# Gated delta rule in a two-block kernel: the block inverse in 64x64 tiles, and the next round's front ordered between the state products

## The reference, cut to what matters

```python
g = jnp.cumsum(g, axis=-1)
decay = jnp.exp(jnp.where(incl, g[..., :, None] - g[..., None, :], -jnp.inf))
kb = k * beta
a_mat = jnp.where(strict, jnp.einsum('bhncd,bhnsd->bhncs', kb, k) * decay, 0.0)
rhs = jnp.concatenate([v * beta, kb * jnp.exp(g)[..., None]], axis=-1)
sol = lax.linalg.triangular_solve(eye + a_mat, rhs, left_side=True, lower=True, unit_diagonal=True)
...
v_new = u_i - jnp.einsum('bhcd,bhdv->bhcv', w_i, state)
o_i = q_i @ state + qk_i @ v_new
state = state * jnp.exp(gl_i)[..., None, None] + jnp.einsum('bhcd,bhcv->bhdv', k_i, v_new)
```

## Time and profile before

| | us |
|---|---|
| median of 3 runs | 2495.45 |
| lowest and highest | 2495.17, 2495.8 |
| the profiled execution | 2499.06 |
| its span | 2497.1 |
| PE busy (share of the span) | 2319.3 (93%) |
| DVE busy | 966.6 (39%) |
| ACT busy | 752.4 (30%) |
| POOL busy | 1029.2 (41%) |
| the recurrence, from the first L1242 to the end of its last product | 322.9 to 674.9 |

### The profile page before, as it was taken

One profiled execution on the slowest core, in us unless ns is written; L12 is line 12 of the kernel. 1 busy time (PEld: TensorE's weight loads), 2 busy tenths in 40 slices (PEclk: granted clock), 3 DMA queues, 4 the chain that ended last, 5 costly groups with the idle time before them and its releaser, 6 DMA issues.

```text
span 2497.1 us, 40813 instructions
## 1 busy us (share of the span) xinstructions
PE 2319.3 (93%) x16316; PEld 1846.6 (74%) x16316; DVE 966.6 (39%) x1715; ACT 752.4 (30%) x1151; POOL 1029.2 (41%) x471
## 2 busy tenths in 40 slices
PE   6998787878798999999999999999999999898999
PEld 2787655666666887887887888887888887547999
DVE  4459554555546122124346112124112113855212
ACT  2443412222223222222222322322322322424444
POOL 1445511132243443443443444443444443303888
PEclk8999776787898999999999999999999999989999
DMA  6233433432452422222432432222432222202555
GB/s 241 93 110 127 152 124 133 161 146 109 178 205 77 169 93 88 98 93 76 154 116 68 160 110 94 93 99 79 143 111 97 97 93 85 73 0 76 186 178 184
DMA packets 82706, 297.78 MB, mean 119 GB/s; under 512 B 9072, under 2 KB 11504, under 8 KB 82288
## 3 DMA queue, kind: packets, MB, share of 16 engines
q1 hardware_dynamic: 82400, 295.03, 34.4%
q10 hardware_dynamic: 144, 0.34, 0.0%
HBM read 294.28 MB, written 1.05 MB: 118 GB/s over the span
## 4 chain that ended last, share of the span: by engine, by line
issue 52%; PE 22%; POOL 19%; DVE 6%; ACT 1%; POOLq 1%; DVEq 0%; ACTq 0%
POOL w_lo L509 19%; PE bank L533 3%; PE bank L534 3%; PE bank L537 3%; PE bank L1292 1%; PE bank L1273 1%; PE bank L577 1%; PE bank L908 1%; DVE gdn_blocks L1510 1%; PE bank L1349 1%; PE bank L2053 1%; PE bank L2054 1%; PE bank L1356 1%; PE bank L2094 1%; PE bank L1281 0%
## 5 line engine op out<-in xcount | busy, mean ns | idle before, releaser
L509 POOL TENSOR_TENSOR w_lo<-w_raw,w_hi 128x1024 fp32r<-128x1024 f32 x383 | 934.3, 2443 | 1181.7 <-ACT w_hi L761 1181.3
L533 PE MATMUL bank<-n_hi,w_lo 128*128 128x512 f32 (+1 forms) x2216 | 796.4, 359 | 38.6 <-POOL w_lo L509 19.5
L537 PE MATMUL bank<-n_lo,w_hi 128*128 128x512 f32 (+1 forms) x2216 | 793.4, 358 | 0.6 <-DVE n_lo L685 0.4
L534 PE MATMUL bank<-n_hi,w_hi 128*128 128x512 f32 (+1 forms) x2216 | 790.4, 357 | 0.0
L761 ACT CAST w_hi<-w_raw 128x1024 fp32r<-128x1024 f32 x383 | 401.1, 1049 | 782.1 <-PE bank L537 771.9
L533 PEld LDWEIGHTS bank<-n_hi,w_lo 128*128 128x128 f32 x2216 | 424.6, 192 | 119.5 <-issue 46.4
L534 PEld LDWEIGHTS bank<-n_hi,w_hi 128*128 128x128 f32 x2216 | 425.0, 192 | 68.2 <-issue 3.6
L537 PEld LDWEIGHTS bank<-n_lo,w_hi 128*128 128x128 f32 x2216 | 424.5, 192 | 66.1 <-DVE n_lo L685 2.6
L1861 DVE TENSOR_TENSOR prod<-silu,bank 128x512 f32<-128x512 f32 (+1 forms) x88 | 54.4, 620 | 731.7 <-PE bank L537 724.3
L537 PE MATMUL bank<-g_lo,w_hi 128*128 128x512 f32 (+1 forms) x768 | 284.6, 371 | 0.0
L533 PE MATMUL bank<-g_hi,w_lo 128*128 128x512 f32 (+1 forms) x768 | 283.0, 369 | 1.1 <-DVE g_lo L1852 1.1
(11 more groups left out here) (314 smaller groups left out, 2018.0 us busy)
## 6 DMA issues: line engine op xcount, KB each, us to landing
w_raw<-in_stream SPq DMA_DIRECT2D x383, 512.0 KB, 3.4
mod_raw<-in_modstream SPq DMA_DIRECT2D x64, 512.0 KB, 4.5
late<-in_modstream SPq DMA_DIRECT2D x56, 512.0 KB, 4.7
w_raw<-in_modstream SPq DMA_DIRECT2D x48, 512.0 KB, 7.0
h<-in_tokens SPq DMA_DIRECT2D x1, 2048.0 KB, 10.7
consts<-in_consts SPq DMA_DIRECT2D x1, 1152.0 KB, 8.6
h<-in_ctx SPq DMA_DIRECT2D x1, 1024.0 KB, 8.2
out<-h SPq DMA_DIRECT2D x8, 128.0 KB, 3.4
```

The lines of the kernel that those rows point to most:

```text
L509: nc.gpsimd.tensor_tensor(w_lo[:, slot, :], w_raw[:, slot, :], w_hi[:, slot, :].bitcast(F32), ALU.subtract).then_inc(w_lo_ready, 1)
L533: nc.tensor.matmul(out_ap, wl, hi, start=start, stop=False)
L534: nc.tensor.matmul(out_ap, wh, hi, start=False, stop=False)
L537: return nc.tensor.matmul(out_ap, wh, lo, start=False, stop=stop)
```

## The change

In the inverse, levels 1 to 4 work on the two 64x64 diagonal blocks instead of the four 32x32 ones. `ac`, `atc`, `xc` and `xtc` are 256 wide instead of 128, and half as many products of twice the size are issued. The first three level masks are applied by DVE (level 1) and POOL (2 and 3, and 4 once the slot of 2 is free). `x_half` and POOL's spreading into `xt` are gone; level 6 reads `xc` and `xtc`, and ACT copies the two diagonal blocks into `xt`. The gram is multiplied by the mask first (from PSUM) and by the decay later (in SBUF).

The next round's front moves into this round: its sums stand behind keys by state, its gram behind the new values, its transposed keys behind the state update, and DVE, ACT and POOL follow. The outputs and the state update now use bank `b0+2`, and the transposed keys `b0`. The slots of the modulation parts in a round are now four, two and six. Of the decay's argument, FWD's is made by ACT (four Relu with a bias of -cum) and BWD's by DVE (subtract, max). The argument for the queries' decay is made by ACT from PSUM.

```diff
-    MOD_SLOTS = {"gram": 6, "at": 0, "level1": 0, "level2": 0, "level3": 0, "level4": 0, "level5": 0, "level6": 0,
-                 "state": 4, "out": 2}
+    MOD_SLOTS = {"state": 4, "out": 2, "gram": 6}
...
+                    at_li = w["ac"] if li == 1 else w["atl"][:, li % 2]
                     for j in range(4):
-                        for i in range(4):
-                            last = nc.tensor.matmul(packed(b0 + 2, blk(i))[:, j], w["atl"][blk(i), li - 1, j],
-                                                    w["xc"][blk(i), j], start=True, stop=True)
+                        for i in range(2):
+                            last = nc.tensor.matmul(packed(b0 + 2, half(i))[:, j], at_li[half(i), j], w["xc"][half(i), j],
+                                                    start=True, stop=True)
...
+        for r, (step_, hg) in enumerate(ROUNDS):
+            inverse(r)
             for n, d, t, hs, b0, gc in batches:
                 if step_:
                     pe.wait_ge(d_state, n - 3)
...
+            if r + 1 < len(ROUNDS):
+                sums(r + 1)
             some_mods(r, "state")
...
+                pe.wait_ge(a_xt, n + 1)
                 four(lambda j: nc.tensor.matmul(b4(b0 + 2)[:, j], w["xt"][:, j], w["rhs"][:, j],
                                                 start=True, stop=True), g_vn)
+            if r + 1 < len(ROUNDS):
+                gram(r + 1)
...
+                    four(out_four, g_o)
             some_mods(r, "out")
...
+                    four(lambda j: nc.tensor.matmul(b4(b0 + 2)[:, j], w["ktok"][:, j], w["rhs"][:, j],
                                                     start=True, stop=True), g_st)
+            if r + 1 < len(ROUNDS):
+                key_rows(r + 1)
+            some_mods(r, "gram")
         mod_turn(pe, RECUR_LAST)

     def act_recur(act):
+        def decay(r):
+            for n, d, t, hs, b0, gc in per_batch(r):
+                if d == BWD:
+                    act.wait_ge(d_relu, r + 1)
+                else:
...
+                        last = nc.scalar.activation(w["dec"][:, j], b4(b0)[:, j], ACT.Relu,
+                                                    bias=neg_cum[:, t, gc.start + j:gc.start + j + 1])
...
+                nc.scalar.activation(w["dec"][:], w["dec"][:], ACT.Exp, scale=-1.0).then_inc(a_dec, 1)
+        def query_decay(r):
...
+                if m >= 2:
+                    act.wait_ge(g_o, m - 1)
+                nc.scalar.activation(w["qdec"][:], b4(b0), ACT.Exp).then_inc(a_qd, 1)
+                for j in range(4):
+                    last = nc.scalar.activation(w["pt"][:, j], b4(b0)[:, j], ACT.Relu, scale=-1.0,
+                                                bias=cum[:, t, gc.start + j:gc.start + j + 1])
...
     def pool_recur(pool):
-                tt(w["atl"][:, 1:4], w["atc"].unsqueeze(1).to_broadcast([P, 3, 4, BLK]),
-                   packed_level[1 - d][:, 2:5].unsqueeze(2).to_broadcast([P, 3, 4, BLK]), ALU.mult).then_inc(p_at, 1)
+                pool.wait_ge(d_a, n + 1)
+                tt(w["atl"], w["atc"].unsqueeze(1).to_broadcast([P, 2, 4, PAIR]),
+                   packed_level[1 - d][:, 1:3].unsqueeze(2).to_broadcast([P, 2, 4, PAIR]), ALU.mult).then_inc(p_at, 1)
-                tt(w["xt"][:].rearrange("p j (i c) -> p j i c", i=4), w["xtc"].unsqueeze(2).to_broadcast([P, 4, 4, BLK]),
-                   own_block.unsqueeze(1).unsqueeze(3).to_broadcast([P, 4, 4, BLK]), ALU.mult).then_inc(p_diag, 1)
...
     def dve_recur(dve):
+        def masked_gram(r):
+                nc.vector.scalar_tensor_tensor(w["a"][:], b4(b0 + 1), -1.0, w["t1"][:],
+                                               ALU.mult, ALU.mult).then_inc(d_gm, 1)
+        def first_blocks(r):
+                dve.wait_ge(d_gm, n + 1)
+                dve.wait_ge(a_dec, n + 1)
+                for i in range(2):
+                    last = tt(w["ac"][half(i)], w["a"][half(i), :, half(i)], w["dec"][half(i), :, half(i)], ALU.mult)
+                step(last)
+                step(tt(w["xc"], w["ac"], first_level[d].unsqueeze(1).to_broadcast([P, 4, PAIR]), ALU.mult))
+                nc.vector.transpose(flat(w["atc"]), flat(w["ac"])).then_inc(d_atc, 1)
+                tt(w["xc"], w["xc"], packed_ident.unsqueeze(1).to_broadcast([P, 4, PAIR]), ALU.add).then_inc(d_xm, 1)
+                tt(w["ac"], w["atc"], packed_level[1 - d][:, 0].unsqueeze(1).to_broadcast([P, 4, PAIR]),
+                   ALU.mult).then_inc(d_at, 1)
+                nc.vector.transpose(flat(w["xtc"]), flat(w["xc"])).then_inc(d_xt, 1)
+                tt(w["a"][:], w["a"][:], w["dec"][:], ALU.mult).then_inc(d_a, 1)
+        def decay_argument(r):
+            n, d, t, hs, b0, gc = per_batch(r)[BWD]
+            step(tt(w["dec"][:], b4(b0), bc(cum[:, t, gc]), ALU.subtract))
+            nc.vector.tensor_scalar(w["dec"][:], w["dec"][:], 0.0, None, ALU.max).then_inc(d_relu, 1)
```

382 lines of the change are left out of this document (205 added, 177 removed).

## The result

The changed kernel takes 2466.8 us (median of 4 runs, 2465.04 to 2467.92) against 2495.62 for the kernel before in the same comparison: a ratio of 0.988, with an interval of 0.9863 to 0.9897. It is 28.8 us faster. The prediction was 2484.6, with a range of 2467 to 2502: the sign was right, but the time lies just under the range, and the gain is more than twice the forecast 10.8.

A forecast was written before the change was run, and what follows sets the result against it. In levels 1 to 4 PE was taken to wait for its instruction stream. Terms -13.2 + 8.1 - 4.8 - 5.6 + 1 + 3.7 = -10.8 us gave 2488.3 for the profiled execution, 2484.6 for the median; range 2467 to 2502.

The forecast's parts named there:

- Levels 1 to 4: Inverse levels in the recurrence: halved instructions should end PE's wait for its instruction stream, 104.0 to 90.8 us, -13.2.
- I take 3.0, the middle: Time per level in levels 1 to 4, taken as 3.0 us between the full-clock and half-clock prices.
- Full clock: Levels 1 to 4 with PE at full clock: the chain bounds a level, at 2.5 us; -27 for the stage.
- Half clock: Levels 1 to 4 at half clock: PE bounds a level, 3.4 us; throughout, as rival, 2498 us, chance 0.17.
- full clock in the levels: Rival: new products keep PE busy 70% or more of a level, stages cost 14 less, 2471 us; chance 0.12.
- Levels 5 and 6: Inverse's last levels: L1535 leaves DVE and L1474 leaves POOL, shortening the way to L1333, -4.8 us.
- First products: Start of each round until both directions have their first block: PE waits for DVE, 39.9 to 48 us, +8.1.
- the front between the state products: Next round's sums, gram and key transposes fill PE's holes between state products, -5.6 us (bounds 0 and -8).
- The charge for collisions: First products: one DVE collision with POOL of 0.85 us a round; as rival, four a round, 2505 us, chance 0.17.
- Modulation parts: Loads for each round's last six parts, now needed some 10 us after the state slot instead of 13: +1 us.
- The joint: Recurrence to output projection: last six parts move behind the outputs, L611 later, squares faster, +3.7 us (0 to +8).
- The backward argument on DVE: BWD's decay argument, about 1.1 us before L1573, covered by four parts and L1356; uncovered 1.1 a round.

The follow-up runs named there:

- the run with the late front: Changed kernel with the next round's sums and gram back behind the state update on all engines, tiles still 64x64: 2466.27 us.
- the run with half the products: Changed kernel with levels 1 to 4 on 32-row tiles, only blocks 0 and 2 of four issued, 128 PE instructions a level: 2492.66 us.
- the small loads: Changed kernel with each modulation load in the recurrence, from the seventh on, bringing 32 of its 1024 columns: 2465.15 us.
- The run with doubled instructions: Changed kernel with every 64x64 product of levels 1 to 4 issued as two of 32 rows, 256 PE instructions a level: 2497.21 us.

## Why the prediction was right or wrong

**Levels 1 to 4** (-13.2, measured -21.3). The place and the wait were right: the break with "issue" is gone, 50 packets became 34, and doubling the instructions again brings both back with the old time. The failed step is "I take 3.0, the middle": a level took 2.7. Both prices it lies between were good. Full clock was priced at 2.5 us a level. Round 3 of the run with the late front, at 1.00, gives 8.8/3.5 = 2.5, and the change itself, at 0.86 to 0.91 in rounds 0 to 3, gives 2.7. Half clock was priced at 3.4, and rounds 0 to 3 of the run with half the products, another kernel, give 11.9/3.5 = 3.4. At that price the stage would have been 101.2 us and not the 104 that the prediction put for the half clock. The clock should have been a case of its own, not an average. The rival "full clock in the levels" (2471) was the one that came nearest, at 0.12. The reason given, that PE would be idle for less of the stage, was also not the whole of it. In the run with half the products PE was never idle in the levels of rounds 0 to 3 and stayed at 0.50; with all of them it was mostly at full clock, breaks or not.

The Trainium skill, "Runtime: NRT & Kernel Launch", section "Instruction fetch mechanics", holds that the fetch is mostly hidden. For a stage in which PE takes 256 small instructions in less than some 3.6 us, the runs here show otherwise.

**Levels 5 and 6** (-4.8, measured -13.0). The missing term is the clock again, which the prediction put at nothing here. At 0.50 throughout, the same code took 46.5 us in the run with half the products (5.8 a round), so the removed L1535 and L1474 are worth some 4 of the 50.8, as forecast. The other 8.7 came with the clock: 0.77 to 1.00 in the change, where before it was 0.50 in seven rounds and 0.67 in the last.

**First products** (+8.1, measured +0.7) and **the front between the state products** (-5.6, measured +6.8). As two terms both are wrong. The error was to price them apart. They are one chain from the new values through DVE's state update and first blocks to the next first product, and when PE comes earlier it waits longer, as the small loads showed (-5.3 and +8.4). Their sum was forecast at +2.5 and measured at +7.5. The front filled nothing: PE was idle in the stretch for 5.6 us before (126.5 less 120.9 busy) and for 5.4 after (133.3 less 127.9), and the whole rise is PE's own busy time. The prediction took that time as unchanged by the order. The sums at their new place took 4.3 us more (21.9 for 17.6), and the modulation parts took longer too (73.0 for 67.2), which was not followed up. Undoing the move changed nothing in the time. The charge for collisions was fair. DVE's first pass, the cut of a block, shows it (minimum, median and maximum in ns):

```profile
L1588 DVE TENSOR_TENSOR gdn_inner<-gdn_a,gdn_dec x32: 404/422/1401, 329.7 to 610.4; 64x256 f32<-64x256 f32 x32
```

Its mean is 691, so the collisions cost 32 x (691 - 422) = 8.6 us in eight rounds, 1.1 a round where I charged 0.85. They lie beside POOL's beta values (L1530) in the first direction and its level masks (L1542) in the second. The 256-wide passes came out at 0.38 to 0.45 us, as taken from the earlier trace rows.

**Modulation parts** (+1). Making the loads small changed the time by 1.7 us in all, less than the runs resolve, and the stretch by 5.3: small, and mostly hidden.

**The joint** (+3.7, measured +4.3): right, in size and in mechanism. L621 (L611 before) starts 9.1 us behind the last product of the recurrence instead of 0.7, and the squares then take 2.50 us, where 2.7 was the estimate and 6.71 the row of before:

```profile
654.94 2.50 DVE L1788 TENSOR_TENSOR qT<-o_sum 128x512 f32<-128x512 f32 x4
```

Changing the order took 4.4 us off the joint.

**Output projection**: no term, -4.5. Its granted clock was 0.92 instead of 0.87, and PE's busy time for the same products 81.8 us instead of 86.9. The run with doubled instructions took 98.6 there. What sets the clock in it was not tested.

**The backward argument on DVE** at no cost: right, as far as the times tell (0.5 us apart).

By stages, the 18 us missing from the sum of -10.8 are 8 in levels 1 to 4, 8 in levels 5 and 6, 2 in keys by state and 4.5 in the projection, all stages in which the granted clock rose, less 5 for the chain. So the mechanism of the main term was right, and what failed is the clock: a middle value in levels 1 to 4 and no term at all elsewhere. What moved it stays open.

## What to carry to other kernels

Where a stage issues many tiny matmuls, divide its time by its packets of instructions: breaks with "issue" at regular places, one a packet, mean that fewer and larger matmuls pay, even when half of what they multiply is zeros. When two limits meet (here the instruction stream at 104 us and the half clock at 102, the latter on a kernel with half the products), removing one shows almost nothing, so price each with the other gone, and treat the two levels of the clock as two cases and not as a mean. Stages that hand over to one another through one engine's chain are costed as one; what pays is to move the work of that chain (DVE's first blocks) to where the engine has room.

## What the runs showed of the hardware

- TensorE at 1.2 GHz while its rows show it busy without a gap: 11.9 us in each of four rounds, and 24.0 us where the same code took 13.2 at 2.4 GHz. A busy share of 100% does not tell the clock; the granted clock must be read.
- Instruction supply of PE: a packet of 256 instructions in 3.6 us on average over the levels, and 3.7 and 4.2 us between two breaks that follow each other. With the DMA engines at a share of 0.02 in the levels the breaks stayed (15.4 us of "issue", 16.2 with the loads).
- Up to about that rate added instructions cost little: 64 more a level cost 6.2 us by the medians, the next 64 cost 24.2.
- A pass of DVE with two SBUF inputs that takes 404 ns at best took up to 1401 beside a POOL operation. The Trainium skill, "SBUF — State Buffer", section "Who interferes with whom", says that these exclude one another; the trace agrees.
